# Four mLSTM heads: a column of ones beside the values, in place of separate products for the denominator

## The reference, cut to what matters

```python
def mlstm_chunkwise(q, k, v, i_pre, f_pre):
    ...
        s = jnp.einsum('bhtd,bhsd->bhts', q_, k_) * dexp
        num = jnp.einsum('bhts,bhsd->bhtd', s, v_) + inter_w[..., None] * jnp.einsum('bhtd,bhde->bhte', q_, C)
        den = jnp.sum(s, axis=-1) + inter_w * jnp.einsum('bhtd,bhd->bht', q_, n)
        h = num / jnp.maximum(jnp.abs(den), jnp.exp(-m_t))[..., None]
```

## Time and profile before

| | |
|---|---|
| median of 3 timed runs | 1326.96 us (1324.94, 1326.96, 1327.00) |
| the profiled execution's own time | 1323.78 us |
| its span, first to last instruction | 1322.1 us |
| PE busy | 1289.8 us, 98% of the span |
| PE weight loads busy | 908.7 us, 69% |
| DVE busy | 695.4 us, 53% |
| ACT busy | 501.6 us, 38% |
| POOL busy | 77.3 us, 6% |

### The profile page before, as it was taken

The page is one execution under the profiler, slowest core; times in us unless marked ns, Lnnn a source line. Parts: engine busy times, 40 slices in busy tenths (PEclk is TensorE's granted clock), DMA queues, the critical chain, the costliest instruction groups (busy, mean ns, idle before and its releaser), DMA issues.

```text
span 1322.1 us, 18062 instructions
## 1 busy us (share of the span) xinstructions
PE 1289.8 (98%) x7214; PEld 908.7 (69%) x7214; DVE 695.4 (53%) x1174; ACT 501.6 (38%) x766; POOL 77.3 (6%) x83
## 2 busy tenths in 40 slices
PE   8999999999999999999999999999999999999998
PEld 7988887976775445444445444459956687799986
DVE  5675668666565222222322222257876877755552
ACT  5555574345242211111111111146414685744442
POOL 5740200100000000000000000000000000000000
PEclk9999999999999999999999999999999999999999
DMA  9653747958865999999999999995505334655540
GB/s 350 229 191 135 254 144 260 368 194 303 308 232 199 396 424 427 427 427 428 428 428 428 427 425 428 427 397 181 180 12 196 139 129 157 195 166 183 192 159 32
DMA packets 101349, 363.68 MB, mean 275 GB/s; under 512 B 4002, under 2 KB 28837, under 8 KB 88912
## 3 DMA queue, kind: packets, MB, share of 16 engines
q1 hardware_dynamic: 97792, 352.86, 68.7%
q0 software_dynamic: 3280, 9.58, 2.2%
q10 hardware_dynamic: 192, 0.06, 0.0%
HBM read 361.43 MB, written 1.05 MB: 274 GB/s over the span
## 4 chain that ended last, share of the span: by engine, by line
PE 84%; DVE 7%; ACT 4%; DMA 2%; issue 2%; ACTq 0%; DVEq 0%
PE bank L510 37%; PE bank L908 15%; PE bank L926 9%; PE bank L883 5%; PE bank L1253 5%; PE bank L939 2%; DVE ring_parts L1301 2%; DMA ring<-in_w 2%; PE bank L835 1%; PE bank L1056 1%; PE bank L916 1%; ACT ring_parts L2119 1%; PE bank L564 1%; DMA ring<-in_w_xkv 1%; PE bank L600 1%
## 5 line engine op out<-in xcount | busy, mean ns | idle before, releaser
L2119 ACT ACTIVATE ring_parts<-ring 128x1024 fp32r<-128x1024 f32 x234 | 242.6, 1057 | 231.5 <-PE bank L510 204.2
L1301 DVE TENSOR_TENSOR ring_parts<-ring,ring_parts 128x1024 fp32r<-128x1024 f32 x214 | 257.3, 1223 | 133.1 <-ACT ring_parts L2119 130.1
L510 PE MATMUL bank<-ring_parts,arena_parts 128*128 128x512 f32 x1056 | 271.7, 392 | 3.6 <-ACT ring_parts L2119 1.5
L510 PEld LDWEIGHTS bank<-ring_parts,arena_parts 128*128 128x128 f32 x1056 | 196.4, 188 | 48.7 <-ACT ring_parts L2119 2.9
L510 PE MATMUL bank<-arena_parts,ring_parts 128*128 128x256 f32 x1504 | 198.0, 284 | 1.2 <-DVE flank_parts L1307 0.7
L909 PE MATMUL bank<-ring,arena 128*64 128x512 f32 x448 | 197.9, 594 | 0.0
L908 PE MATMUL bank<-ring,arena 128*64 128x512 f32 x432 | 190.7, 594 | 6.1 <-issue 6.1
L510 PEld LDWEIGHTS bank<-arena_parts,ring_parts 128*128 128x128 f32 x1504 | 190.1, 192 | 2.1 <-DVE flank_parts L1307 0.8
L908 PEld LDWEIGHTS bank<-ring,arena 128*64 128x64 f32 x432 | 57.4, 137 | 125.3 <-issue 125.3
L510 PE MATMUL bank<-ring_parts 128*128 128x512 f32 (+1 forms) x624 | 117.2, 346 | 2.1 <-DVE ring_parts L1301 1.2
L926 PE MATMUL bank<-ring,arena 128*64 128x512 f32 x448 | 113.4, 595 | 1.1 <-DMA ring<-in_w 1.1
(11 more groups left out here) (385 smaller groups left out, 1440.0 us busy)
## 6 DMA issues: line engine op xcount, KB each, us to landing
ring<-in_w SPq DMA_DIRECT2D x83, 2048.0 KB, 20.4
ring<-in_w_in SPq DMA_DIRECT2D x27, 2048.0 KB, 9.4
flank<-in_w SPq DMA_DIRECT2D x13, 2048.0 KB, 20.7
ring<-in_w_ada SPq DMA_DIRECT2D x12, 2048.0 KB, 8.0
ring<-in_w_ffn_gate SPq DMA_DIRECT2D x11, 1024.0 KB, 5.4
ring<-in_w_ffn_up SPq DMA_DIRECT2D x11, 1024.0 KB, 8.0
ring<-in_w_ffn_down SPq DMA_DIRECT2D x5, 2048.0 KB, 7.9
ring<-in_w_xkv SPq DMA_DIRECT2D x4, 2048.0 KB, 16.3
```

The source lines that it names most:

```text
L510: mm = pe.matmul(ps[:, o:o + width], *pair, start=(o == 0 and kk == 0 and ha + hw == 0), stop=(kk == kn - 1 and (ha, hw) == terms[-1] and ...
L1301: dve.tensor_tensor(low, src, high, ALU.subtract).then_inc(low_ready, 1)
L2119: act.activation(high, src, ACT.Copy).then_inc(high_ready, 1)
```

## The change

The values lie in blocks of 257 columns: 256 values of one head and a column that holds 1.0. A pair (token tile t, half j) has two heads, thus two blocks. Three of the four pairs lie in `arena` from 4096 on (6 blocks, 1542 columns), and the fourth (t = 1, j = 1) lies in row 2 of `rows`. POOL writes the columns of ones once at the start, behind its other memsets. One product of 257 columns takes the place of the two products. As row 2 is now in use until the last head is done, the two b_gate loads stand behind the wait for the last head's banks.

```diff
-        V = tiles(4096, NT, D)
+        VW = DH + 1
+        V_three = arena[:, 4096:4096 + 6 * VW].rearrange("p (b n) -> p b n", n=VW)
+        V_last = rows[:, 2, 0:2 * VW].rearrange("p (b n) -> p b n", n=VW)
+
+        def V(t, j):
+            i = 2 * t + j
+            return V_three[:, 2 * i:2 * i + 2, :] if i < 3 else V_last
...
             def weighted(h):
                 emptied(pe, f"s{h}")
                 if h == 0:
+                    pe.wait_ge(s["v_ones"], 2)
                     emptied(pe, *jobs_of("v", 2, 2))
                 for t in range(NT):
                     ps = take(f"num{h}{t}")
-                    for c0, c1, rhs in ((0, DH, None), (DH, DH + 1, ones[:, 0:1])):
-                        for st in range(t + 1):
-                            o = t * P if st == 0 else 256
-                            mm = pe.matmul(ps[:, c0:c1], PR[:, o:o + P],
-                                           V[:, st, h * DH:(h + 1) * DH] if rhs is None else rhs,
-                                           start=(st == 0), stop=(st == t))
+                    for st in range(t + 1):
+                        o = t * P if st == 0 else 256
+                        mm = pe.matmul(ps[:, 0:VW], PR[:, o:o + P], V(st, h // 2)[:, h % 2, :], start=(st == 0), stop=(st == t))
                     give(f"num{h}{t}", mm)
...
-                    did(act.activation(V[:, t, j * 512:(j + 1) * 512], ps[:], ACT.Copy), free(nm))
+                    did(act.activation(V(t, j)[:, :, 0:DH], ps[:].rearrange("p (h n) -> p h n", h=2), ACT.Copy), free(nm))
...
             pool.memset(scT[:, :, 2:32], 0.0).then_inc(s["consts"], 1)
 
+            for v in (V_three, V_last):
+                pool.memset(v[:, :, DH], 1.0).then_inc(s["v_ones"], 1)
             pool.dma_start(wif[:], ...
...
             full(pool, "ifcols")
             emptied(pool, "ifcols")
+            for t in range(NT):
+                full(pool, f"num{H - 1}{t}")
             for i in range(2):
                 pool.dma_start(rows[:, 2 + i, :], w["b_gate"][:, i * D:(i + 1) * D].broadcast_to([P, D])).then_inc(s["rowsp_in"], 16)
-            for t in range(NT):
-                full(pool, f"num{H - 1}{t}")
 
             pool.dma_start(memhat, w["mem"][0].rearrange("(t p) n -> p t n", p=P)).then_inc(s["mem_in"], 16)
```

More of the change, by code:

```diff
@@ L341, in two_blocks @@
                      "route_exp route_in rows1_in rows2_in rowf_in rows_g rowsh_in rowsp_in sheet1_in sheet2_in silu_c "
-                     "gut_silu dft_in pool_low upped wroute_in x0_in x1_in x_new xexp xmax ").split():
+                     "gut_silu dft_in v_ones pool_low upped wroute_in x0_in x1_in x_new xexp xmax ").split():
             s[name] = sem(name)
```

## The result

The changed kernel takes 1332.06 us (median of 18 runs, 1327.24 to 1335.42) against 1326.99 us for the kernel before in the same runs: ratio 1.0038, 95% interval 1.0029 to 1.0048. One run of the kernel before took 2641.63 us, twice the others, and has no part in the ratio. The forecast was 1324.0, with a range that ended at 1326.9, and a chance of 0.04 for slower. The profiled execution took 1333.05 us.

A forecast was written before the change was run, and what follows sets the result against it. TensorE (PE) was taken as the bound, busy nearly all the time; 2.4 us saved in the heads gave 1324.6 us from the median and 1323.3 from the mean, so 1324.0 was forecast, range 1322.2 to 1326.9.

The forecast's parts named there:

- What goes, in PE's time: In the four heads, dropping the ones products saves PE 3 x 0.57 + 0.68 = 2.4 us.
- the seam's loss: Behind three heads, the next score row's changed weight shape takes back about 0.09 us of the saving each.
- Rival B: In the heads, ones are cheap because weight loads pace PE: only 0.6 us goes, 1325.8 us; 5%.
- What is added and moved: 257th column 0.02 us; memsets, split copies, pitch and later b_gate loads at nothing; first DMA up to 0.5 us later.
- rival C: Value products at a pitch of 257 slow down from odd starts: about level at +2.3 us, or 1329.8; 6%.
- What is late next: After the heads, from 174 us on, later work and loads move with PE, so all 2.4 us reach the end.
- The clock: Whole kernel: PE's clock is at 2.4 GHz throughout, so no part of the argument is about it.
- The sum: Whole time: 1323.8 - 2.4 = 1321.4 profiled, 1324.6 from the median, 1323.3 from the mean; 1324.0 taken.
- rival D: Nothing lost at the seams and better load phase in the DMA-bound stage: -3.5 us, 1322.6 us; 12%.
- Rival A: From 207 us on, a weight or GpSimd load keeps its own time and swallows the 2.4 us: 1326.9 or 1325.7; 12%.

The follow-up runs named there:

- e3: Changed kernel with its whole layout, but separate products for values and ones, restoring PE's old program length: 1326.82 us, ratio 0.9997 to the kernel before.
- e6: Changed kernel with 8 padding instructions at the head of PE's program: 1331.58 us in one run, beside 1326.30 for the kernel before.
- e2: Kernel before with only the products with the column of ones left out, layout unchanged: 1330.82 us, ratio 1.0022 to the kernel before.

## Why the prediction was wrong

- **What goes, in PE's time: right.** 0.57 us per head and the seam's loss were forecast; 1.95 - 1.39 = 0.56 was measured, 2.3 us over four heads against 2.4. Rival B, that only 0.6 us goes, is refuted. The first products behind the heads started at 145.76 and the load of mem at 147.83, not at 144.2 and about 146 as forecast, since this execution came to the heads 1.5 us late from a half-clock stretch at 42 us.
- **What is added and moved: right.** Memsets, pitch (rival C) and the late b_gate loads were costed at nothing, and e3 shows 0.9997, with up to 1.6 us not excluded. For the pitch alone the starts 0.216 us apart leave nothing to rival C. The first DMA moved by 0.07 us, not up to 0.5.
- **What is late next: wrong.** The step that failed is the sentence "No source of work in the path has a time of its own. I expect all of the 2.4 us at the end." It looked at semaphores and at the loads of data. PE's own program is also a stream of loads, and what it needs at 883 us depends on how many instructions stand in front, not on when they run. The 48 removed instructions put the branch's target two pieces away, and in place of 2.4 us gained at the end there was a stand of 5.7 us at 883 and 2.6 us of half clock behind it. No rival had this.
- **The clock: wrong.** "No part of the argument is about it" held for the execution that I read, which was a lucky one: its mean granted clock was 0.999, and its 1323.78 us lie below all of the timed runs of the kernel before. The stall made it an argument: 2.6 us of the loss, read in the starts at 0.43 us against 0.23.
- **The sum.** 5.7 + 2.6 - 2.3 = +6.0 us; measured between the medians +5.1 (interval 1.0029 to 1.0048, 3.8 to 6.4 us). The other 3.2 us of the profiled execution, at 42 and 872 us, are half-clock stretches that come and go from run to run (below). Two slips in the prediction change nothing: rival D's -3.5 us is 1322.8 between median and mean, not 1322.6, and a run of 257 words in its lines of four words touches 65 lines from any start, never 66.
- **Rival A**, a swallowed gain, has the right sign of doubt and the wrong mechanism: the gain was not swallowed, it arrived at 871.6 and was then lost to a stall and the half clock behind it, 8.3 us together.

What the profile of before did show: the page's queue of instructions with 60 transfers, one row of 477 ns for the branch, and a jump over 338 instructions, more than one piece. The Trainium skill, "Runtime: NRT & Kernel Launch", section "Instruction fetch mechanics", says that instructions come in 16 KiB blocks of 256, that prefetch is sequential, and that a taken branch whose target is outside a window of two pages stalls for a fetch. The traces agree, with 6.2 us as the price here. The same section of the Trainium skill gives PE room for 2048 instructions. If PE kept that room filled ahead, there would by an estimate from this figure have been no stall, and the time would have been the forecast's; the runs show no such use of it, as a target 338 on stalled PE.

## What to carry to other kernels

Before counting an edit of a long unrolled program as a gain, look for taken branches behind it that jump over more than one piece of instructions. Adding or removing instructions in front, or inside a body that never runs, can move the target over the edge of a piece, at 6 us a time under full DMA load, and more where the clock falls behind it (8.3 us here). Such a kernel is best measured with its length padded both ways: here the change alone is +0.4%, and with 24 or 48 idle instructions at the start it is faster than both kernels, 0.9967 and 0.9977.

## What the runs showed of the hardware that was not expected

The kernel's time from run to run goes with its clock. Of 35 runs of the kernel before, the three with a mean granted clock of 0.999 have a median of 1324.6 us, the eight at 0.998 have 1325.6, the seven at 0.995 have 1329.5. One stretch at half clock lies within 40 to 46 us in the changed kernel, behind 3.6 us of matmuls of 8 columns (L631); the same stretch of before ran at full clock.

```profile
37.88 3.64 PE L631 MATMUL bank<-wif,flank 128*128 128x8 f32 x32
```

```profile
40.00:46.00 6.00, 6.00 (x40) 6.00 (x40) 4.04 (x10) 0.82 (x2) 1.57 (x1) 0.72 1.05 386
```

Before:
```profile
40.00:46.00 6.00, 6.00 (x53) 6.00 (x53) 4.02 (x10) 2.23 (x4) 1.82 (x2) 1.00 1.05 387
```

Such a stretch, which begins during the matmuls of 8 columns or up to 1.5 us behind the last, is in ten of the twelve traces that are kept, and not in those of before and e6. It is not the same in every execution of one kernel either: of e2's two profiled executions one came to the first head at 99.92 us and the other, with the stretch, at 101.49. So neither layout nor length decides it. What does stays open; a longer matmul in place of those of 8 columns was not tried. It also means that two single traces can't be subtracted as they stand: 3.2 of the 9.2 us between the two shown here are such stretches.
